# A fourth slot for split weights in the memory of the cross keys and values, and the small steps between stages in another order

## What is computed

```python
x = x + cross_attention(rms_norm(x, g_cross), rms_norm(mem, g_mem), w_cq, w_ckv, w_co)
u = rms_norm(x, g_mlp) @ w_up                      # 1024 -> 4096
x = rms_norm(x + square(relu(u)) @ w_down, g_final)
for l in range(2):
    h = rms_norm(x, norm_g[l, 0]) * (1 + sc1) + sh1      # shift, scale, gate from c @ ada_w + ada_b
    x = x + 0.5 * g1 * (silu(a) * b) @ w2                # a, b = split(h @ w13), 2816 wide
    ...                                                  # mixer, gated by g2
    ...                                                  # second SwiGLU, gated by 0.5 * g3
return rms_norm(x, final_g)
```

## Time and profile before

| | us |
|---|---|
| median of 3 runs | 1575.82 (1574.57 to 1583.59) |
| the profiled execution | 1585.44 |
| its span, first to last instruction | 1583.7 |
| PE busy | 1470.7 (93%) |
| PE weight loads busy | 1216.0 (77%) |
| DVE busy | 1070.5 (68%) |
| ACT busy | 727.0 (46%) |
| DMA | 314 MB, mean 198 GB/s |

### The profile page before, as it was taken

One profiled execution on the slowest core, in us unless ns is written; L12 is line 12 of the kernel. 1 busy time (PEld: TensorE's weight loads), 2 busy tenths in 40 slices (PEclk: granted clock), 3 DMA queues, 4 the chain that ended last, 5 costly groups with the idle time before them and its releaser, 6 DMA issues.

```text
span 1583.7 us, 18472 instructions
## 1 busy us (share of the span) xinstructions
PE 1470.7 (93%) x7116; PEld 1216.0 (77%) x7116; DVE 1070.5 (68%) x1438; ACT 727.0 (46%) x1064; POOL 67.7 (4%) x109
## 2 busy tenths in 40 slices
PE   4988789899999999989889999899998989899998
PEld 3776667788887888878778888688887868688886
DVE  3687675667677766776657666777767778676445
ACT  5444454544436434454454333444334756353443
POOL 4000000000001000010000000000000000000000
PEclk9999899999999999999699999999999999899999
DMA  7753052577766777846148779678776630475651
GB/s 250 257 204 112 28 181 84 187 265 266 277 228 194 264 263 261 265 165 180 55 158 290 251 257 255 207 241 283 256 238 214 179 110 1 133 241 171 208 187 70
DMA packets 189116, 314.25 MB, mean 198 GB/s; under 512 B 6960, under 2 KB 100455, under 8 KB 189031
## 3 DMA queue, kind: packets, MB, share of 16 engines
q1 hardware_dynamic: 148528, 231.82, 45.5%
q10 hardware_dynamic: 38678, 76.69, 13.4%
q0 software_dynamic: 1824, 4.57, 0.9%
HBM read 311.99 MB, written 1.07 MB: 198 GB/s over the span
## 4 chain that ended last, share of the span: by engine, by line
PE 79%; DVE 9%; ACT 4%; issue 3%; POOL 2%; DMA 2%; ACTq 0%; DVEq 0%; POOLq 0%
PE ps L998 23%; PE ps L1000 23%; PE ps L999 22%; PE ps L1007 5%; PE ps L1297 2%; DVE wlo L958 2%; PE ps L1134 1%; PE ps L1252 1%; ACT whi L949 1%; DVE xn L1704 1%; DMA qT<-in_ada_w 1%; DVE tmp L1738 1%; DVE rmax L2029 1%; DMA raw<-in_nsa_w_out 1%; DVE sp L2026 1%
## 5 line engine op out<-in xcount | busy, mean ns | idle before, releaser
L958 DVE TENSOR_TENSOR wlo<-raw,whi 128x2048 fp32r<-128x2048 f32 (+1 forms) x221 | 501.6, 2271 | 179.9 <-ACT whi L949 179.2
L998 PE MATMUL ps<-whi,aT 128*128 128x512 f32 (+1 forms) x1216 | 493.5, 406 | 36.3 <-DVE aTl L1726 28.1
L1000 PE MATMUL ps<-wlo,aT 128*128 128x512 f32 (+1 forms) x1216 | 480.4, 395 | 0.0
L999 PE MATMUL ps<-whi,aTl 128*128 128x512 f32 (+1 forms) x1216 | 479.6, 394 | 0.0
L949 ACT ACTIVATE whi<-raw 128x2048 fp32r<-128x2048 f32 (+1 forms) x221 | 418.7, 1895 | 118.9 <-PE ps L1000 81.1
L998 PEld LDWEIGHTS ps<-whi,aT 128*128 128x128 f32 x1216 | 234.6, 193 | 85.0 <-issue 41.2
L1000 PEld LDWEIGHTS ps<-wlo,aT 128*128 128x128 f32 x1216 | 234.2, 193 | 49.7
L999 PEld LDWEIGHTS ps<-whi,aTl 128*128 128x128 f32 x1216 | 235.3, 193 | 43.7
L998 PE MATMUL ps<-whi,hT 128*128 128x512 f32 (+1 forms) x524 | 200.2, 385 | 2.2 <-ACT z L1537 1.4
L1000 PE MATMUL ps<-wlo,hT 128*128 128x512 f32 (+1 forms) x524 | 197.4, 379 | 0.0
L999 PE MATMUL ps<-whi,hTl 128*128 128x512 f32 (+1 forms) x524 | 197.0, 378 | 0.0
(11 more groups left out here) (230 smaller groups left out, 1296.4 us busy)
## 6 DMA issues: line engine op xcount, KB each, us to landing
raw<-in_ff_w SPq DMA_DIRECT2D x176, 512.0 KB, 4.8
...
```

The costliest lines, as they stand in the source:

```text
L958: dve.tensor_tensor(wlo[:, slot, 0:m], raw[:, slot, 0:m], whi[:, slot, 0:m].bitcast(F32), ALU.subtract).then_inc(w_lo, 1)
L998: pe.matmul(out_ap, hi, w, start=start, stop=False)
L999: pe.matmul(out_ap, lo, w, start=False, stop=False)
L1000: return pe.matmul(out_ap, hi, wl, start=False, stop=stop)
```

## The change

The 32 KB per partition behind `zc` get a second name, `wide`: a fourth slot for a high and a low part. It is in use from the edge after cross attention on, except from the third unit of the hybrid mixer's input product to the end of that mixer, where `zc` holds other things. The last gain moves from `zc` to `kz`. Slots are no longer taken in turn: each unit takes the one that was used longest ago. The plan marks the points at which splits may be made (`tick`), each with the last unit that PE has used up by then, and gives each point at most two splits that are free to be made.

At an edge:

- The rounding of chunks 0 to 3 and their low parts are done in two pairs, each with its own count; the rounding of the first pair starts when DVE has scaled two chunks.
- Of the adds of tile 1 only the first half comes ahead of the scaling of tile 0's chunks where the branch is gated.
- The second unit's split is no longer made in the edge where the fourth slot let it be made before (all but the first edge and the one ahead of the cross query; in the edges after attention its low part comes between the adds of tile 0 and the scaling).
- The steps of tile 1 come six matmuls later: after the first two chunks of the second unit.
- In `edge_post` ACT splits its unit after the chunks of tile 1, where it was ahead of them.
- In the last edge DVE multiplies x by the gain before the inverse root is there, and ACT takes three of the four last products.

The diff, cut:

```diff
-LEAD = RING - 1
+WIDE = RING + 1
...
+        self.slots.append(dict(n=WIDE if self.wide else RING, zc=self.zc_left))
         return len(self.units) - 1
+
+    def tick(self, done, upto=None):
+
+        self.ticks.append((done, upto, []))
+        return self.ticks[-1][2]
+
+    def place_splits(self):
+
+        last, zc = [None] * WIDE, None
+        for u, s in enumerate(self.slots):
+            s["slot"] = min(range(s["n"]), key=lambda i: -1 if last[i] is None else last[i])
+            s["last"] = last[s["slot"]]
+            last[s["slot"]] = u
+            s["zc"] = s["zc"] if s["slot"] == RING and s["zc"] != zc else None
+            zc = s["zc"] or zc
+        n = 0
+        for done, upto, out in self.ticks:
+            while n < len(self.units) and len(out) < 2 and (upto is None or n <= upto) and (
+                    self.slots[n]["last"] is None or self.slots[n]["last"] <= done):
+                out.append(n)
+                n += 1
+        assert n == len(self.units)
...
+            self.left[c] = ("edge", st["lo0"] + 1 + min(c // 2, 2))
+        a = len(self.units)
+        st["first"] = self.tick(0, 0) if acc is None else []
+        st["late"] = self.tick(a - 2 if a else 0, a + 1)
+        st["acc_splits"] = (acc or {}).get("splits")
         st["turns"] = [self.rounds(2, ["D", "A"])]
         self.edge_open = self.stage("edge", **st)
 
-    def edge_post(self, late):
+    def edge_post(self, b):
         st, self.edge_open = self.edge_open, None
-        st["late"] = late
         st["turns"].append(self.rounds(2, ["D", "A"]))
-        return dict(kind="edge_post", edge=st, u=late - 1)
+        return dict(kind="edge_post", edge=st, splits=self.tick(b - 2, b + 1))
...
-                e += [up(0, fills, (0,), split=False), ("stage", post), up(1, fills, (0,), split=False),
-                      up(0, fills, (1,), split=False)]
+                e += [up(0, fills, (0,)), up(1, fills, (0,), cs=range(2)), ("stage", post),
+                      up(1, fills, (0,), cs=range(2, 4)), up(0, fills, (1,))]
                 mark_up(0, fills)
                 e += self.ada_unit()
-                e.append(up(1, fills, (1,), split=True))
+                e.append(up(1, fills, (1,), splits=self.tick(us[1] - 1)))
                 mark_up(1, fills)
                 e += self.ada_unit()
...
-    p.edge(p.out_rest(out[0]), ("prm", G_MLP), eps=1e-5)
+    acc = p.out_rest(out[0])
+    p.wide, p.zc_left = True, (p.groups[-1]["fill"], 0)
+    p.edge(acc, ("prm", G_MLP), eps=1e-5)
...
-            p.linear(A["hy_w_in_2"][0], D, 1952, "z", "hy_in", flush=3,
+            p.linear(A["hy_w_in_2"][0], D, 1952, "z", "hy_in", flush=3, wide=2,
...
+            p.wide, p.zc_left = True, (p.groups[-1]["fill"], 1)
...
+        with nc.sbuf_tensor("zc", [P, NT, 2048], F32) as zc:
+            pass
+        wide = sb("wide", [2, UNIT], F32R)
         vcb = kz[:, 10:12, :]
+        gain = kz[:, 0:4, :].rearrange("p a b -> p (a b)")
...
+        def split_hi(act, units):
+
+            for u in units:
+                act.wait_ge(w_raw[u % RING], arrived[u])
+                if p.slots[u]["last"] is not None:
+                    wait_used(act, lambda j: p.slots[u]["last"], 0)
+                if p.slots[u]["zc"]:
+                    fill, conv = p.slots[u]["zc"]
+                    act.wait_ge(u_ready, fill + 1)
+                    if conv:
+                        act.wait_ge(conv_done, 1)
+                act.activation(hi_of(u), raw_of(u), ACT.Copy).then_inc(w_hi, 1)
+
+        def split_lo(dve, units):
+
+            for u in units:
+                dve.wait_ge(w_hi, u + 1)
+                dve.tensor_tensor(lo_of(u), raw_of(u), hi_of(u).bitcast(F32), ALU.subtract).then_inc(w_lo, 1)
...
+                                if post and (i, tt, k) == (1, 0, 2):
+                                    handle(post)
...
-            def edge_high(tt, q):
-                act.activation(aT[:, 4 * q:4 * q + 4, tt * P:(tt + 1) * P], tmp[:, q, :].rearrange("p (a b) -> p a b", b=P),
+            def edge_high(c0, n, tt):
+                act.activation(aT[:, c0:c0 + n, tt * P:(tt + 1) * P],
+                               tmp[:, c0 // 4, (c0 % 4) * P:(c0 % 4 + n) * P].rearrange("p (a b) -> p a b", b=P),
                                ACT.Copy).then_inc(nhi_ready, 1)
 
             def edge_q0(st, tt):
 
-                t = st["turns"][tt][0]
-                wait_emptied(act, T, lambda j: t)
-                edge_high(tt, 0)
+                act.wait_ge(xt_ready, st["xt0"] + tt + 1)
+                edge_high(0, 2, tt)
+                wait_emptied(act, T, lambda j: st["turns"][tt][0])
+                edge_high(2, 2, tt)
...
                 if st["rescale"]:
                     edge_squares(st, "g", 0)
                     edge_squares(st, "x", 0)
-                    edge_squares(st, "g", 1)
+                    edge_squares(st, "g", 1, (0,))
+                    edge_scale(st, 0)
+                    edge_squares(st, "g", 1, (1,))
                 else:
                     edge_squares(st, "x", 0)
-                if st["acc"] is None:
-                    split_hi(act, lambda j: 0)
-                elif not st["rescale"]:
-                    split_hi(act, lambda j: st["late"])
-                edge_scale(st, 0)
-                if st["acc"] is None:
+                    split_hi(act, st["first"])
+                    edge_scale(st, 0)
+                    if st["acc"] is None:
+                        edge_squares(st, "x", 1)
+                    else:
+                        split_hi(act, st["late"])
+                        edge_squares(st, "x", 1, (0,))
+                edge_q0(st, 0)
+                edge_q1(st, 0)
+                if st["rescale"]:
                     edge_squares(st, "x", 1)
-                edge_q0(st, 0)
-                if st["rescale"]:
-                    split_hi(act, lambda j: st["late"])
-                if st["acc"] is not None:
-                    edge_squares(st, "x", 1)
-                edge_q1(st, 0)
-                if st["acc"] is None:
-                    split_hi(act, lambda j: st["late"])
+                elif st["acc"] is None:
+                    split_hi(act, st["late"])
                     act.wait_ge(t_dve, 1)
                     act.activation(cact[:, :], prm[:, C_COL:C_COL + KC], ACT.Silu).then_inc(cact_ready, 1)
+                else:
+                    edge_squares(st, "x", 1, (1,))
 
             def edge_post(st):
                 edge_scale(st["edge"], 1)
-                split_hi(act, lambda j: st["u"] + LEAD)
                 edge_q0(st["edge"], 1)
                 edge_q1(st["edge"], 1)
+                split_hi(act, st["splits"])
...
-            def edge_low(tt, q):
-                hi, lo = [t[:, 4 * q:4 * q + 4, tt * P:(tt + 1) * P] for t in (aT, aTl)]
-                dve.tensor_tensor(lo, tmp[:, q, :].rearrange("p (a b) -> p a b", b=P), hi.bitcast(F32),
-                                  ALU.subtract).then_inc(nlo_ready, 1)
+            def edge_low(st, k, c0, n, tt):
+                hi, lo = [t[:, c0:c0 + n, tt * P:(tt + 1) * P] for t in (aT, aTl)]
+                dve.wait_ge(nhi_ready, st["hi0"] + 3 * tt + k + 1)
+                dve.tensor_tensor(lo, tmp[:, c0 // 4, (c0 % 4) * P:(c0 % 4 + n) * P].rearrange("p (a b) -> p a b", b=P),
+                                  hi.bitcast(F32), ALU.subtract).then_inc(nlo_ready, 1)
 
             def edge_q0(st, tt):
 
                 t = st["turns"][tt][0]
                 dve.wait_ge(t_ready, t + 1)
-                if st["lo0"] + 2 * tt > 0:
-                    dve.wait_ge(nlo_ready, st["lo0"] + 2 * tt)
+                if st["lo0"] + 3 * tt > 0:
+                    dve.wait_ge(nlo_ready, st["lo0"] + 3 * tt)
                 for c in range(4):
                     scale, shift = edge_args(st, c)
                     args = (scale, None, ALU.mult) if shift is None else (scale, shift, ALU.mult, ALU.add)
                     ins = dve.tensor_scalar(tmp[:, 0, c * P:(c + 1) * P], tbank(t)[:, c * P:(c + 1) * P], *args)
+                    if c == 1:
+                        ins.then_inc(xt_ready, 1)
                 ins.then_inc(t_dve, 1)
-                dve.wait_ge(nhi_ready, st["hi0"] + 2 * tt + 1)
-                edge_low(tt, 0)
-
-            def edge_q1(st, tt):
-
-                dve.wait_ge(nhi_ready, st["hi0"] + 2 * tt + 2)
-                edge_low(tt, 1)
+                for k in range(2):
+                    edge_low(st, k, 2 * k, 2, tt)
+
+            def edge_last(st):
+                for h in range(2):
+                    edge_add(st, 0, h)
+                for h in range(2):
+                    edge_gain(st, 0, h)
+                for h in range(2):
+                    edge_add(st, 1, h)
+                for h in range(2):
+                    edge_gain(st, 1, h)
+                dve.wait_ge(rstd_ready, st["x"]["rstd"][1])
+                dve.wait_ge(xg_ready, 3)
```

(29 more changed lines are left out.)

210 lines of the change are left out of this document (103 added, 107 removed).

## The result

| | before | changed |
|---|---|---|
| median of 4 runs each, one chip, us | 1576.04 | 1606.33 |
| range, us | 1574.57 to 1583.59 | 1604.6 to 1610.73 |
| span of the profiled execution, us | 1583.7 | 1605.4 |

The ratio of changed to before is 1.0162 (95% interval 1.013 to 1.0194). The change is slower by 1 to 2%; I had forecast 0.5%. In the later groups three executions took 2.9 to 5.1 ms (one each of the kernel before, of three slots and of the changed kernel again); they stand in the medians and in no ratio.

A forecast was written before the change was run, and what follows sets the result against it. PE, busy 93% of the span, was taken as the bound, with only its ten edges open to gain. Gains of 20.1 against costs of 28.5 us net +8.4, so 1575.8 becomes 1584.2 us; range 1571 to 1592.

The forecast's parts named there:

- step 6: Behind tile 1's transposes only six matmuls cover its chain: PE waits 0.4 us at nine edges, 3.6 us longer.
- 1, 2: chunk pairs, second add: Edges: paired rounding shortens nine chains, 8.6 us gained; tile 1's second gated add leaves the path at gated edges, 5.4.
- 3: clock kept at two edges: At the two gated edges after attention PE's idle shrinks from 3.43 to 1.7 us, keeping full clock: 3.3 us gained.
- 4: wait for tile 1's norm: PE's 0.76 us wait goes at two ungated edges after attention, plus 0.5 at the first edge: 2.0 us gained.
- 5: last edge: At the last edge one product on DVE beside others on ACT replaces a pair: 0.8 us gained, perhaps about 0.4.
- 7: starved first step, idle only: First step of five MLPs: extra splits delay the products, PE waits about 4 us in each, 21.3 us longer in sum.
- bracket: clock falls at the new idle: Behind the new 2.9 us idle in five MLPs the clock might fall: 0 to 8.5 us more, set at nothing.
- bracket: clock back earlier at four edges: At four edges keeping their low clock, full speed might return a step earlier: 0 to 6.8 us less, set at nothing.
- 8 and all else in products with attention: Products that are no MLP: splits come late or stand ahead of a bank's evacuation, 3.6 us longer in sum.
- rival B: Clock falls at every MLP's new idle and never returns earlier elsewhere: +17 us, 1593, over 1% slower; chance 0.10.
- The fourth slot itself costs nothing: Mid-stage the fourth slot keeps the same instructions, sizes and rhythm one unit further ahead; no cost, no wait to remove.
- Rival C: At edges, the second unit's split was never on the path; held true, otherwise 1 to 2 us less; no chance given.

The follow-up runs named there:

- three slots: The changed kernel with the fourth slot never used, so the second unit is split in the edge again: 1586.66 us, ratio 1.0016 to the kernel before.
- the kernel with one split: The changed kernel, but only one split ahead of tile 1's product in each MLP's first step: 1586.17 us, ratio 1.002 to the kernel before.
- with 12: Tile 1's steps back after 12 matmuls: 1582.76 us (ratio 0.9984) with the fourth slot and one split ahead of the product, 1588.89 (1.0028) without the slot.

## Why the prediction was wrong

It failed in its net, by 13 us in the traces (+8.4 forecast, +21.7 found). By its own steps, each read from the two traces but for step 6, which is from the experiments:

| step | forecast | found |
|---|---|---|
| 1, 2: chunk pairs, second add | -14.0 | -14.0 |
| 3: clock kept at two edges | -3.3 | -3.3 |
| 4: wait for tile 1's norm | -2.0 | -0.8 |
| 5: last edge | -0.8 | -0.8 |
| 6: six matmuls | +3.6 | about 3 |
| 7: starved first step, idle only | +21.3 | +15.9 |
| bracket: clock falls at the new idle | 0 | +9 |
| bracket: clock back earlier at four edges | 0 | -3.0 |
| not foreseen: late in the third SwiGLU | 0 | +3.5 |
| 8 and all else in products with attention | +3.6 | +9.0 |

The 0.8 of step 4 is 2.06 us of waits that are gone, as forecast, less a new one of 1.31 for tile 1's low parts at the first edge. The found column sums to 18.5. Of the second bracket 1.6 lie at the hybrid and sparse edges and are in the last row as well; another 1.6 us of the 21.7 stay unassigned.

No single row makes the 13 us. The terms that were sized wrong are the clock (+6.0), the products with attention (+5.4) and the idle late in the third SwiGLU (+3.5), and item 7's idle, sized too large, hides 5.4 of them.

**The step that failed** is "I set both at nothing: they have opposite signs, like sizes". The clock fell at all five idle spans, once for two stretches, and what came back at four edges was a third of that: windows of 5 us read 0.71, 0.66, 0.67 and 0.66 where they had read 0.50 to 0.55, 0.6 to 0.85 us each. (That gain is one trace pair's: the second traces read 1.00, 0.50, 0.66 and 1.00 in the changed kernel and 0.67, 0.71, 0.60 and 0.50 in the kernel before.) The bound that stood for the lower end was no bound. The rows gave 2.42 as kept and 3.43 as lost, but in the second trace of the same kernel the same 2.42 at the same two edges is followed by 0.59 and 0.57. One execution in which the clock is kept says only that it can be. In the midst of an MLP it was lost behind idle of 1.70, 1.75 and 1.88 us and of 2.25 to 2.93 in 14 cases of 15, and kept behind 1.77, 2.51 and 2.54, among others. So the length of the idle does not decide it by itself; what else does is not shown. The first half of rival B, to which I gave 0.10, is what happened (its second half, that the clock never comes back earlier elsewhere, did not in this pair), and on top of it came:

**Transfers.** Not in any step: a gate's small pieces and a modulation load. The sparse stage was 5.6 us longer, 3.2 in the second trace of the changed kernel (165.9 and 163.5; the kernel before has 160.3 and 160.2). Item 8 had 1.4 for it. The gate's transfer meets the output weights in the kernel before as well; there PE waits 1.9 and 1.5 us at the place where it waits 4.1 and 5.2 now. So the change made PE wait for the collision. Which of its edits did is open: the stage is long with three slots too (162.8, 165.0), so the slot is not needed for it. Late in the third SwiGLU DVE waits longer for a modulation load than the 2.7 us it waited before, and PE behind it:

```profile
1199.22 0.49 DVE L1994 TENSOR_SCALAR qT<-qT,cact 128x512 f32<-128x512 f32 x1 [4.30 <-DMA qT<-in_ada_w]
```

```profile
1200.98 0.47 PE L1062 MATMUL ps<-whi,hT 128*128 128x512 f32 x1 [1.75 <-DVE hTl L2047]
```

The clock reads 0.57 over the next 4 us, behind only 1.75 us of idle. Holding that gate back only moved the idle; the cause there is not shown.

**Item 7's size.** The chain on DVE and ACT came out within 0.2 us at every point, and the kernel with one split shows that it is the cause. It was sized 5.4 us too large: PE waits 0.3 to 0.7 for the first product in four MLPs and not at all in the third SwiGLU, where I had 1.1, and 2.5 to 2.9 for the second. In the first SwiGLU PE's own row of work was 1.0 longer than my sum, 0.5 of it the modulation's small matmuls. That the undersized clock and the oversized idle nearly cancel is luck.

**"The fourth slot itself costs nothing", and gives nothing.** The first half held. The second held with six matmuls, as in the change (1.0016 without the slot, 1.002 with it), and failed with 12, where it is worth 6 to 7 us. Rival C was judged on the old chain; once the chain is shorter, the split in the edge is next in line, by way of ACT's queue at one edge and of POOL's step at the gated ones. The prediction saw the second of these ("POOL's 1.37 at an edge lies under a split that the change removes there") and gave it no term of its own. The question "what is late next" was asked for PE's first matmul, not for chunks 4 to 7 and tile 1.

**Item 5 and the shared port.** The end of the changed kernel, where the earlier trace rows show before:

```profile
1599.43 1.29 DVE L1826 TENSOR_TENSOR z<-x,kz 128x512 f32<-128x512 f32 x2
...
1600.18 2.11 ACT L1508 ACTIVATE xn<-z,rstd 128x512 f32<-128x512 f32 x3
1600.37 0.52 POOL L2389 TENSOR_SCALAR ms<-ss 128x1 f32<-128x1 f32 x1 [4.27 <-ACT xn L1459]
```

From the last add to the last product it took 3.59 us and takes 2.78. POOL's step is recorded from 1600.37, while DVE's second product (two SBUF inputs) runs until 1600.72, and ends 0.17 us behind it; beside an idle DVE the same step took 0.30 us in the trace before. The rule of the Trainium skill ("SBUF — State Buffer", "two separate sides"), that one of the two waits out the other's instruction, fits this; but the product was half over, so of the 0.4 us that I named for it 0.2 at most were paid. Nor was that new: in the kernel before the same step lay beside DVE's last products of tile 0 and took 0.64, so against it the change lost nothing here, and item 5's gain came out at the full 0.8. The steps of 1.90 us at the gated edges with three slots, shown with the experiments, fit the rule far better.

**The baseline.** The two medians differ by 30.3 us, the two traces by 21.7. The second trace of before goes with it: its execution took 1576.42 where the first profiled one took 1585.44, and 8.2 us of that are clock in the hybrid mixer, which the first trace lost. By 17 to 35 runs in each later group the kernel before is at 1583 to 1584, and the changed one, in the last group, 18 us above it by the ratio.
